# A recurrent scan's beginning in a new order: first pair's products on VectorE, first chunk in two stages

## What is computed

```python
def rwkv7_scan(r, w, k, v, kk, bb, s0, reverse):
    def step(s, inp):
        r_t, w_t, k_t, v_t, kk_t, b_t = inp
        sa = jnp.einsum('bhij,bhj->bhi', s, kk_t)
        s = s * w_t[:, :, None, :] - sa[..., None] * b_t[:, :, None, :] + v_t[..., None] * k_t[:, :, None, :]
        return s, jnp.einsum('bhij,bhj->bhi', s, r_t)
```

## Time and profile before

| | |
|---|---|
| median of 3 runs | 3516.14 us (3513.63 to 3526.28) |
| the profiled execution | 3518.56 us, its span 3516.8 us |
| TensorE busy | 3212.9 us (91%) |
| VectorE busy | 1626.2 us (46%) |
| ScalarE busy | 1194.6 us (34%) |
| GpSimd busy | 1342.6 us (38%) |
| the scan phase | from 2317 to 2954 us of the span |

### The profile page before, as it was taken

How to read it: one execution, slowest core, us unless ns; L and a number is a source line. 1 busy time by engine, 2 the same in 40 slices (tenths; PEclk the granted TensorE clock), 3 DMA queues, 4 the chain that set the end, 5 groups by cost and what they waited for, 6 DMA issues and landing times. The chain is left out here.

```text
span 3516.8 us, 49237 instructions
## 1 busy us (share of the span) xinstructions
PE 3212.9 (91%) x18471; PEld 2593.2 (74%) x18471; DVE 1626.2 (46%) x3082; ACT 1194.6 (34%) x2125; POOL 1342.6 (38%) x877
## 2 busy tenths in 40 slices
PE   6999988899998999898999959985988999989996
PEld 5888765688877888676788848873766777768875
DVE  6444386444435653412711044326666645264443
ACT  3222245322223222343322232243444434243342
POOL 3444431344443443333344423242666630133332
PEclk8999989899998999899999979996999999979998
DMA  7555321355544545222433332222222233112211
GB/s 228 187 178 173 112 76 35 120 185 181 171 132 156 175 135 159 76 78 66 141 95 92 98 113 60 70 80 61 49 51 45 62 85 106 36 48 60 60 49 42
DMA packets 636826, 363.03 MB, mean 103 GB/s; under 512 B 109182, under 2 KB 629108, under 8 KB 636144
## 3 DMA queue, kind: packets, MB, share of 16 engines
q1 hardware_dynamic: 632432, 353.48, 34.2%
q10 hardware_dynamic: 3056, 6.29, 0.5%
q0 software_dynamic: 1168, 0.91, 0.1%
HBM read 334.12 MB, written 26.50 MB: 103 GB/s over the span
## 5 line engine op out<-in xcount | busy, mean ns | idle before, releaser
L266 POOL TENSOR_TENSOR w_lo<-w_raw,w_hi 128x1024 fp32r<-128x1024 f32 (+1 forms) x398 | 939.8, 2362 | 1735.7 <-ACT w_hi L258 1735.7
L303 PE MATMUL acc<-h,w_hi 128*128 128x512 f32 x3136 | 978.7, 393 | 6.4 <-POOL w_lo L266 6.4
L258 ACT ACTIVATE w_hi<-w_raw 128x1024 fp32r<-128x1024 f32 (+1 forms) x398 | 414.4, 1042 | 996.5 <-PE acc L303 960.9
L303 PEld LDWEIGHTS acc<-h,w_hi 128*128 128x128 f32 x3136 | 584.0, 188 | 128.5 <-POOL w_lo L266 7.5
L303 PE MATMUL acc<-h,w_lo 128*128 128x512 f32 x1568 | 613.4, 391 | 0.0
L303 PE MATMUL acc<-hid,w_hi 128*128 128x512 f32 x1408 | 437.2, 392 | 0.0
L303 PE MATMUL lat<-h,w_hi 128*128 128x512 f32 x912 | 336.6, 407 | 16.0 <-DVE h L428 13.8
L303 PEld LDWEIGHTS acc<-h,w_lo 128*128 128x128 f32 x1568 | 295.0, 188 | 63.7
L707 DVE SCALAR_TENSOR_TENSOR ada_part<-ada_raw,c_act,ada_part 128x256 f32<-128x256 f32 x672 | 314.9, 488 | 18.6
L303 PEld LDWEIGHTS acc<-hid,w_hi 128*128 128x128 f32 x1408 | 263.6, 188 | 54.3
L303 PE MATMUL acc<-hid,w_lo 128*128 128x512 f32 x704 | 275.1, 391 | 0.0
(11 more groups left out here) (495 smaller groups left out, 5001.3 us busy)
## 6 DMA issues: line engine op xcount, KB each, us to landing
w_raw<-in_ffn_w SPq DMA_DIRECT2D x240, 512.0 KB, 3.9
ada_raw<-in_ada_w SPq DMA_DIRECT2D x88, 1024.0 KB, 5.0
w_raw<-in_od_w_in SPq DMA_DIRECT2D x32, 512.0 KB, 4.0
w_raw<-in_ev_w_in SPq DMA_DIRECT2D x30, 512.0 KB, 3.8
w_raw<-in_ffn_w SPq DMA_DIRECT2D x32, 384.0 KB, 3.4
image<-inverse_wait SPq DMA_DIRECT2D x288, 32.0 KB, 2.1
first_ada<-in_ada_w SPq DMA_DIRECT2D x8, 1024.0 KB, 12.3
w_raw<-in_ab_w_in SPq DMA_DIRECT2D x16, 512.0 KB, 3.9
```

The lines of the kernel that those rows point to most:

```text
L258: act.activation(K.w_hi[:, first % SPLIT, 0:tiles, :], K.raw[:, first % RAW, 0:tiles, :], ACT.Copy).then_inc(K.hi_ready, 1)
L266: pool.tensor_tensor(K.w_lo[:, first % SPLIT, 0:tiles, :], K.raw[:, first % RAW, 0:tiles, :], K.w_hi[:, first % SPLIT, 0:tiles, :].bitcast ...
L303: mm = pe.matmul(out, w[:, slot, k, :], moving(ap, k, tokens), start=first and k == 0 and p == 0, stop=last and k == tiles - 1 and p == le ...
```

## The change

- VectorE does the twelve products of pair 0 (`products`), between its own pieces 14, 25 and 31. GpSimd only splits weights 2 to 4 there. TensorE starts the six low products of pair 0 at place 26 of its multiplies rather than 33, and the bonus product of pair 0 (`prepare(0, 29)`) is at place 36 rather than behind the multiplies. ScalarE copies the low products ahead of `late(3)`.
- Pair 0's inversion on VectorE stands behind piece 8 of pair 1, its turning on ScalarE at 13 rather than 17, ahead of the two rates.
- The first chunk is in two stages. TensorE, ScalarE: pieces 0 to 16 of pair 1, then both stages. VectorE: pieces 0 to 8, first stage (`take`, `keys`), pieces 9 to 16, second stage (`cross`, `join`, `turn`).
- Pieces 17 to 35 of pair 1 go into the first ten slots of pair 0, two in each. The low products of pair 1 start at slot 10, its turning is in slot 30, and the 36 pieces of pair 2 share slots 10 to 35: piece 23 is in slot 27.
- SyncE reads the images of chunk 3 of pair 0 ahead of the sends of pair 1.

```diff
-        def blocks(prepare, invert, begin, step):
-            for n in range(23):
+        def blocks(prepare, invert, begin, step, early=17):
+            for n in range(early):
                 invert(0, n)
                 prepare(1, n)
-            begin()
-            for n in range(23, NCH * SLOTS):
+            begin(0)
+            for n in range(early, 17):
                 prepare(1, n)
+            begin(1)
             for b in range(RB):
                 for k in range(NCH):
                     def between(slot, b=b, k=k):
                         n = SLOTS * k + slot
+                        if b == 0:
+                            for m in range(17 + 2 * n, min(19 + 2 * n, NCH * SLOTS)):
+                                prepare(1, m)
+                            if n >= 10:
+                                invert(1, n - 10 if n != 30 else 27)
+                                for m in range((n - 10) * 36 // 26, (n - 9) * 36 // 26):
+                                    prepare(2, m)
+                            return
...
@@ SyncE @@
                     images(b, 2)
+                    if b == 0:
+                        images(b, 3)
...
-                    for k in range(3, NCH):
+                    for k in range(3 if b else 4, NCH):
...
@@ GpSimd @@
-                prepare(0, split)
+                for seg, i, _ in LATE[SPLIT:]:
+                    split_lo(pool, K, seg, i, i, 0, DB)
                 pool.wait_ge(K.chunks_done, LATE_DONE)
-                pool.wait_ge(S.pq, len(PREP["pool"]))
...
@@ TensorE @@
-                def begin():
-                    ready(0)
-                    pe.wait_ge(S.cleared, 2)
-                    pe.wait_ge(S.late_ready, len(LATE))
-                    for part in chunk_parts((0, 0)):
+                def begin(stage):
+                    if stage == 0:
+                        ready(0)
+                        pe.wait_ge(S.cleared, 2)
+                        pe.wait_ge(S.late_ready, len(LATE))
+                    for part in chunk_parts((0, 0))[3 * stage:3 + 4 * stage]:
...
-                        if 33 <= place < 33 + 2 * PAIRS:
-                            invert(0, place - 33)
+                        if 26 <= place < 26 + 2 * PAIRS:
+                            invert(0, place - 26)
+                        if place == 36:
+                            prepare(0, 29)
...
-                prepare(0, 29)
@@ ScalarE @@
-                    if n == (27 if c else 17):
+                    if n == (27 if c else 13):
...
-                late(3)
                 for n in range(2 * PAIRS):
                     invert(0, n)
+                late(3)
                 late(4)
@@ VectorE @@
+                    def products(n):
+                        def op(out, a, b, alu, *waits):
+                            for engine, what in waits:
+                                dve.wait_ge({"act": S.pa, "dve": S.pd, "pool": S.pq}[engine], prep(engine, 0, what))
+                            dve.tensor_tensor(out, a, b, alu).then_inc(S.pq, 1)
+                        q, rate = O.q, O.rate
+                        if n == 14:
+                            for d in range(2):
+                                op(q[d], O.cs[d], q[d], ALU.subtract, ("dve", f"sum{d}"))
+                            op(kk, kk, tmp, ALU.mult, ("dve", "inv"))
+                        if n == 25:
+                            op(tmp, O.kt[0], O.kt[1], ALU.add, ("dve", "k1"), ("pool", "kk"))
+                            for d in range(2):
+                                op(rate[d], rate[d], kk, ALU.mult, ("dve", f"kt{d}"), ("pool", "kk"))
+                                op(rate[d], rate[d], wi[d], ALU.mult, ("act", f"wi{d}"), ("pool", f"bkk{d}"))
+                            for d in range(2):
+                                op(q[d], q[d], kk, ALU.mult, ("act", f"q{d}"))
+                        if n == 31:
+                            for d in range(2):
+                                op(O.kt[d], O.kt[d], wi[d], ALU.mult, ("pool", "ksum"))
...
-                    if c or n != 6:
+                    if c or n != 8:
...
-                blocks(prepare, invert, begin, step)
+                blocks(prepare, invert, begin, step, 9)
```

More of the change, by code:

```diff
@@ L2156, in invert, with prepare @@
                     pool.sem_inc(S.solved, 1)
-                def prepare(c, split=lambda name: None):
+                def prepare(c):
                     def op(name, out, a, b, alu, *waits):
-                        split(name)
                         for engine, what in waits:
@@ L2519, in state_parts, with begin @@
                     return right, solve
-                def begin():
-                    for part in chunk_parts((0, 0)):
+                def begin(stage):
+                    for part in chunk_parts((0, 0))[stage:1 + 2 * stage]:
                         part(0)
@@ L2629, in prepare @@
                             done(dve.tensor_tensor(O.cs[d], O.cs[d], row(0), ALU.mult))
+                    if c == 0:
+                        products(n)
                     if n == 26:
@@ L2691, in clear, with begin @@
                     dve.wait_ge(S.reset, b * 2 + 2)
-                def begin():
+                def begin(stage):
                     dve.wait_ge(S.tables, 80)
-                    for part in chunk_parts((0, 0)):
+                    for part in chunk_parts((0, 0))[2 * stage:2 + 3 * stage]:
                         part(0)
```

## The result

The changed kernel takes 3533.35 us (median of 20 runs, 3524.07 to 3541.70) against 3519.38 us for the kernel before in the same measurement (20 runs): ratio 1.0043, 95% interval 1.0032 to 1.0053, so 11 to 19 us slower.

A forecast was written before the change was run, and what follows sets the result against it. Bound by a serial chain before the first step, then pair 0's chain from pair 1's last low copy: first `rhs` 12.7 us earlier, pair 1's first `rhs` 12.4 later, so 3516.14 becomes 3528.5 us; range 3503 to 3540.

The forecast's parts named there:

- Inversion of pair 0 ends: Before the first step, on VectorE: the inversion ends at 2402.0 in the profile's clock rather than 2409.8.
- ScalarE's square for pair 1: Before the first step: it waits for the last output's transfer, so this chain stays, at 2386.1 in the profile's clock.
- First `rhs`: Start of pair 0's step 0: at 2435.0 in the profile's clock, 12.7 us earlier than 2447.70; bounds 9 and 16.
- Steps 0 and 1: Pair 0's first two steps, with pair 1's remaining 19 pieces packed in: 17 and 14.5 us.
- Last low copy: Pair 1's last low product, in slot 15 of pair 0: copied by about 2474.5, against 2463.1 before.
- From copy to `before0`: In pair 0, from pair 1's last low copy through GpSimd's inversion to pair 2's `before0`: 48.1 us.
- The wait in slot 27: Step 4 of pair 0: ScalarE stands 11 to 12 us before the exponential on `before0`.
- From the turning to pair 1's first `rhs`: End of pair 0, from turning pair 1's blocks through memory and image reads to pair 1's first step: 23.0 us.
- Pair 1's first `rhs`: Start of pair 1's first step: at 2553.0 in the profile's clock, 12.4 us later than 2540.62.
- Rival 1: The beginning's gain stays, with pair 1's last low copy before 2462: 3506 to 3510 us; chance 0.22.
- Rival 3: Before the first step, low products not brought forward, `q0` late: start gains 5 rather than 12.7, 3536 us; chance 0.08.
- rival 2: Pair 0's packed steps take 18 us, VectorE and GpSimd in turn, also a falling clock: last copy 2480, 3535; chance 0.22.

The follow-up runs named there:

- kernel 3: The changed kernel with pair 2's `before0` and `before1` done by VectorE right behind its sums instead of GpSimd: ratio 1.0016 to the kernel before.

## Why the prediction was right

It said 3528.5 us, 12.4 more than its median of before; the two medians measured together differ by 14.0, the ratio by 15. The time lies within the range, 0.35 us above the 3521 to 3533 to which I gave 0.48. The signs it named are there: VectorE idle 9.07 us behind the inversion (some 10), ScalarE idle 9.81 before an exponential (over 8), the second inversion's end at 2516.7, that is 196.9 after the start, against some 203.7 (2521 less 2317.3). Step by step, in us from the phase's start (predicted, found):

- Inversion of pair 0 ends: 84.7, 82.7. The stop of 1.83 us behind the first copy was there, at half the rate for one pair of products after it, and cost less than the 3.0 I put in: two products at distances of 2.69 and 2.58 us for 1.91, 1.5 us in all.
- ScalarE's square for pair 1: 68.8, 65.1; it waited only for the output's transfer. I had TensorE's last multiply too late. It didn't matter, as the turning waits for the inversion.
- First `rhs`: 117.7, 113.6. I gave the products and the two stages 12.7 us of gain together, they had 16.8. From `y` to the first `rhs` it was 8.5 us, near the 8.3 I had, but VectorE came to `y` 4.3 us earlier.
- Steps 0 and 1: 17 and 14.5, 14.9 and 14.6. Packing pair 1's pieces was cheap: 19 of them, with two low products, cost 7.5 us over two bare steps of 11.0.
- Last low copy: 157.2, 151.4. This is the largest miss, 5.8 us: 4.1 of it from the first `rhs`, 2.1 from step 0; I charged a slow clock to step 0 that was there for part of it (0.88 granted in the mean).
- From copy to `before0`: 48.1, 47.5. The wait in slot 27: 11 to 12, 9.8. From there to the turning: 7.4, 8.6.
- From the turning to pair 1's first `rhs`: 23.0, 26.9. This term was mis-sized the other way. I took before's distance, where `rhs` of step 5 fell well behind the turning, its image wait was 1.2 us, and step 5 went on beside the transfers. Now step 5 has just begun when the turning starts, and TensorE stands 10.3 us.
- Pair 1's first `rhs`: 235.7, 234.5.

So the mechanism held and the sum was near, partly as two misses of 4 to 6 us went opposite ways. Rival 1 is out: the copy came at 151.4, not before 144.7, its point. Rival 3 is out: the last low product came 10.4 us earlier, counted from the phase's start. Of rival 2 the price on the last copy is out: steps 0 and 1 took 14.9 and 14.6 us, not 18. Its falling clock is there: between 2537.6 and 2544.0, behind the 8.27 us stop in step 5, the windows view grants 0.50. Its mechanism is visible too. In step 0 a state update of VectorE with a median of 0.35 us over eighteen of its kind lasts 1.77 and ends 0.15 us behind the GpSimd product that began just before it (1.81 us), and a copy of 6 columns lasts 1.78 and ends with another. From the timelines of VectorE and of GpSimd in the changed kernel:

```profile
2441.12 1.77 DVE L2715 SCALAR_TENSOR_TENSOR state<-state,w_last,const 128x128 f32<-128x128 f32 x1
...
2445.56 1.78 DVE L2654 COPY w_last<-q_r_rate 128x6 f32<-128x6 f32 x1
```

```profile
2440.93 1.81 POOL L2173 TENSOR_TENSOR q_r_rate<-q_r_rate,x_context 128x768 f32<-128x768 f32 x1
2442.70 1.86 POOL L2173 TENSOR_TENSOR q_r_rate<-q_r_rate,x 128x768 f32<-128x768 f32 x1
2444.70 2.60 POOL L2173 TENSOR_TENSOR q_r_rate<-q_r_rate,w_inv 128x768 f32<-128x768 f32 x1
```

That is what the Trainium skill, page "SBUF — State Buffer", section "SBUF: two separate sides", says of the port pair of these two engines, held by one for a whole instruction; the trace agrees. But what it cost was not 5 us in the last copy: step 0 was shorter than forecast, and I take it that most of these instructions were not on the step's own chain, though no run shows that.

Three small slips stand in the working. The last copy's sum gives 2474.8 and not 2474.5, the lower end 2462.0 and not 2462.3. And the VectorE product of 0.96 us in the earlier trace rows did not have the memory to itself: a product of GpSimd began 0.08 us behind it and took 2.57 us, not 1.85, so VectorE had only come first. None of them moves the forecast by more than 0.3 us.

```profile
2358.64 2.57 POOL L2163 TENSOR_TENSOR q_r_rate<-q_r_rate,w_inv 128x768 f32<-128x768 f32 x1
```

What stays open: 4.7 of the 14.5 us between the two profiled spans lie outside the scan phase, where the code is the same. The changed kernel's twenty executions span 17.6 us, so I put it down to that; no run tests it. Why steps 2 and 3 of the changed kernel take 43 us together, 21 over bare, was not taken apart by a kernel either. The timeline shows that in step 3 VectorE works on pair 2's sums and keys from 2484.36 to 2502.08 without a pause (18.35 us busy in 22.1; before, the same work is spread over steps 1 and 2, with 9.88 us busy in 18.2 and 14.27 in 18.0), and TensorE waits 2.7 us for VectorE's `x` there. In the changed kernel the chain hides this: ScalarE still waits 9.81 us in step 4. Shorter steps 2 and 3 would first have made that wait longer.

## What to carry to other kernels

In an order written out by hand, look for the longest chain from each producer to its last consumer before moving either. A short wait of a late consumer (1.43 us here) says that the chain behind it is as long as all that hides it; what a producer's move adds in slots must then be set against what is won ahead of it. And an instruction that only unblocks a transfer (the turning) belongs ahead of those that wait for the same event for other ends: 2 us of work moved by three slots were worth 8.0 us at pair 1's first `rhs`, and some 13 by the ratios.

## What the runs showed that I had not expected

- Two waits of 9.8 and 10.3 us on one path, each removable by itself for 7 to 8 us in the profile, give no more together (228.1 against 226.5 and 227.5).
- Starting a group of low products two slots earlier made the step 4.9 us longer and its end no earlier.
- TensorE took 2.93 us for a small product right after 8.68 us of idle time, and 1.56 for its like ten us before. The granted clock was 0.50 in the first stretch and 1.00 in the second, the clock's two levels, 1.2 and 2.4 GHz. This stop cost 1.4 us more, in this one product, than its length.
- Taking one consumer out of the inversion's way (`before0` in kernel 3) brought out the next, `ksum`, with a wait of 7.01 us.
